# FFN 0 of a layered fp32 backbone on Trainium2: the up projection of seven feature pieces as seven block products

## The reference

```
h = x * (1 + scale) + shift
x = LayerNorm(alpha * x + gate * f(h))          # f: the mixer, then the MLP
_sq_relu_mlp(h, w1, w2) = square(relu(h @ w1)) @ w2      # 1024 -> 4096 -> 1024
```

## Time and profile before

| | us |
|---|---|
| median of three runs | 1986.85 (1986.79 to 1987.31) |
| the profiled execution | 1987.33 |
| its span, first to last instruction | 1985.5 |
| TensorE busy | 1974.4 (99%) |
| VectorE busy | 1257.6 (63%) |
| ScalarE busy | 627.3 (32%) |
| GpSimd busy | 435.5 (22%) |

### The profile page before, as it was taken

One profiled execution on the slowest core, in us unless ns is written; L12 is line 12 of the kernel. 1 busy time (PEld: TensorE's weight loads), 2 busy tenths in 40 slices (PEclk: granted clock), 3 DMA queues, 4 the chain that ended last, 5 costly groups with the idle time before them and its releaser, 6 DMA issues.

```text
span 1985.5 us, 26120 instructions
## 1 busy us (share of the span) xinstructions
PE 1974.4 (99%) x9693; PEld 1696.7 (85%) x9693; DVE 1257.6 (63%) x1783; ACT 627.3 (32%) x897; POOL 435.5 (22%) x350
## 2 busy tenths in 40 slices
PE   9999999999999999999999999999999999999998
PEld 6889889889989988998888888888888888888887
DVE  4756678688656745565783644553554477776778
ACT  3413222144222222222444223313322334444443
POOL 0300311324331233243350020020020026200004
PEclk9999999999999999999999999999999999999999
DMA  9613334332423422333322121212112125877646
GB/s 340 239 64 75 117 117 138 97 96 96 147 97 116 127 95 95 127 125 128 88 95 69 53 91 64 75 64 80 63 65 90 55 85 168 225 218 194 173 147 148
DMA packets 84640, 235.51 MB, mean 119 GB/s; under 512 B 14144, under 2 KB 27072, under 8 KB 84416
## 3 DMA queue, kind: packets, MB, share of 16 engines
q1 hardware_dynamic: 77104, 212.00, 31.9%
q0 software_dynamic: 5616, 18.35, 5.2%
q10 hardware_dynamic: 1824, 3.85, 0.6%
HBM read 219.99 MB, written 2.12 MB: 112 GB/s over the span
## 4 chain that ended last, share of the span: by engine, by line
PE 95%; POOL 1%; DVE 1%; DMA 1%; SPq 1%; issue 1%; ACT 1%; POOLq 0%; ACTq 0%; DVEq 0%
PE bank L863 21%; PE bank L865 21%; PE bank L864 21%; PE bank L901 7%; PE bank L903 7%; PE bank L902 7%; PE bank L1439 2%; PE bank L1442 2%; PE bank L1441 2%; PE bank L1216 1%; PE bank L1167 1%; PE bank L1079 1%; DMA mod<-mod_units_d 0%; PE bank L1051 0%; PE bank L1101 0%
## 5 line engine op out<-in xcount | busy, mean ns | idle before, releaser
L1865 DVE TENSOR_TENSOR w_lo<-raw,w_hi 128x1024 fp32r<-128x1024 f32 x185 | 246.2, 1331 | 325.8 <-ACT w_hi L1465 325.6
L1465 ACT ACTIVATE w_hi<-raw 128x1024 fp32r<-128x1024 f32 x185 | 195.2, 1055 | 561.9 <-PE bank L865 349.2
L863 PE MATMUL bank<-hT_hi,w_hi 128*128 128x384 f32 (+1 forms) x992 | 341.9, 345 | 0.0
L865 PE MATMUL bank<-hT_hi,w_lo 128*128 128x384 f32 (+1 forms) x992 | 340.5, 343 | 0.0
L864 PE MATMUL bank<-hT_lo,w_hi 128*128 128x384 f32 (+1 forms) x992 | 340.5, 343 | 0.0
L2645 POOL TENSOR_TENSOR res_lat<-res_lat,gy 128x512 f32<-128x512 f32 x112 | 149.3, 1367 | 515.3 <-DVE gy L1974 414.9
L901 PE MATMUL bank<-w_hi,hT_hi 128*128 128x512 f32 x592 | 230.6, 389 | 0.0
L902 PE MATMUL bank<-w_lo,hT_hi 128*128 128x512 f32 x592 | 230.3, 389 | 0.0
L903 PE MATMUL bank<-w_hi,hT_lo 128*128 128x512 f32 x592 | 230.3, 389 | 0.0
L863 PE MATMUL bank<-w_hi,act_hi 128*128 128x512 f32 x504 | 198.2, 393 | 0.0
L865 PE MATMUL bank<-w_hi,act_lo 128*128 128x512 f32 x504 | 196.5, 390 | 0.0
(11 more groups left out here) (346 smaller groups left out, 3485.9 us busy)
## 6 DMA issues: line engine op xcount, KB each, us to landing
raw<-w_units_d SPq DMA_DIRECT2D x249, 512.0 KB, 3.3
mod1a<-mod_units_d SPq DMA_DIRECT2D x32, 384.0 KB, 3.8
mod1b<-mod_units_d SPq DMA_DIRECT2D x32, 384.0 KB, 4.1
wsum<-w_units_d SPq DMA_DIRECT2D x24, 512.0 KB, 3.4
bv<-mod_units_d SPq DMA_DIRECT2D x16, 512.0 KB, 3.4
mod<-mod_units_d SPq DMA_DIRECT2D x14, 512.0 KB, 8.2
wsum<-w_units_d POOLq DMA_DIRECT2D x12, 512.0 KB, 7.9
wsum<-wsum POOLq DMA_DIRECT2D x12, 512.0 KB, 5.9
```

The lines of the kernel that those rows point to most:

```text
L863: nc.tensor.matmul(out, s_hi, m_hi, start=first, stop=False)
L865: return nc.tensor.matmul(out, s_lo, m_hi, start=False, stop=last)
L1465: nc.scalar.activation(halves_of(phase, k, i)[0], raw[:, s, :], ACT.Copy).then_inc(hi_done, 1)
L1865: tt(lo, raw[:, s, :], f32(hi), ALU.subtract).then_inc(lo_done, 1)
```

## The change

1. **Seven products.** In the seven later pieces the up projection is a 2 x 2 by 2 x 2 block product (inputs and features of the weights in two halves, inputs and tokens of the activations in two halves) made with seven products in place of eight. Product q: two feature blocks j, 4 input blocks, three matmuls each, 24 of 384 columns; the order is q1, q6, q5, q3, q7, q2, q4, where q2 and q4 add to the open banks of q1 and q7.
2. **Weight sums.** Four of the seven weight operands are T1 to T4, running sums of blocks, made by accumulate DMAs from GpSimd's queue in three slots `wsum0`. A piece has 11 splits in place of 8.
3. **Token operands.** s1, s2, s4 and q7's operand are sums of blocks of the activations, made once in ffn0a: ScalarE copies three blocks' high halves (x21, x22, x11), six accumulate DMAs of 384 KB add the low halves, VectorE sums (`operand0_sum`) and ScalarE and VectorE split the sums (`operand0_hi`, `operand0_lo`). s4 needs four more DMAs.
4. **Combines.** VectorE makes the results from banks and two common sums: `common`, `less_common` and `result` (14 operations of 384 columns and six squares with relu), with ScalarE's relu for q2.
5. **Modulation.** Four slots (mod1); each piece's products go in four or five places of VectorE's order (MOD1_PLACES: 1, 1, 2, 2, 2 in the mixed pieces, 2, 2, 2, 2 in ffn0z); `rows0` stands behind the third unit of the down half in `ffn0`, `cols0` two tiles later.
6. **Residual.** The 12 shift additions become six accumulate DMAs of 512 KB, each issued behind its pair of multiplications in ffn0a. In the heads ScalarE waits for the residual ahead of the copy of the first score.
7. Loops are unrolled; buffers and parities of slots move accordingly.

The core of the diff:

```diff
+PRODUCTS0 = [(1, 6, True), (6, 0, True), (5, 2, True), (3, 0, True), (7, 4, True), (2, 6, False), (4, 4, False)]
...
+MOD1_SEQ = [(g, n) for g in range(PIECES_MIXED) for n in range(KC)]
+for _p, _a, _b in ((3, 0, 2), (4, 2, 5), (5, 5, 8)):
+    MOD1_SEQ += [(_p, n) for n in range(KC)] + [(7, n) for n in range(_a, _b)]
+MOD1_SEQ += [(6, n) for n in range(KC)]
+MOD1_PLACES = [[1, 1, 2, 2, 2]] * 3 + [[1, 2, 2, 2, 3]] + [[1, 2, 2, 3, 3]] * 2 + [[2, 2, 2, 2]]
...
+            def ffn0(p):
+                phase, i = piece0(p)
+                for n, (q, b, opens) in enumerate(PRODUCTS0):
+                    pe.wait_ge(lo_done, before("splits", phase, i) + n + 1)
+                    if p == 0 and q in SLO:
+                        pe.wait_ge(s_lo0, SLO[q])
+                    hi, lo = halves_of(phase, n, i)
+                    x_hi, x_lo = OPERANDS0[q]
+                    for j in range(2):
+                        free(phase, i, f"q{q}.{j}")
+                        out = bank[b + j][:, 0:HALF0]
+                        for kc in range(KC // 2):
+                            w = slice((j * KC // 2 + kc) * P, (j * KC // 2 + kc + 1) * P)
+                            nc.tensor.matmul(out, hi[:, w], x_hi[:, kc, :], start=opens and kc == 0, stop=False,
+                                             skip_group_check=True)
+                            nc.tensor.matmul(out, hi[:, w], x_lo[:, kc, :], start=False, stop=False, skip_group_check=True)
+                            last = nc.tensor.matmul(out, lo[:, w], x_hi[:, kc, :], start=False, stop=kc == KC // 2 - 1,
+                                                    skip_group_check=True)
+                        last.then_inc(pe_step, 1)
...
+                def rows():
+                    pe.wait_ge(mod_used, len(MOD1_SEQ) if phase == "ffn0z" else MOD1_SEQ.index((p, KC - 1)) + 1)
+                    mod_sums(phase, i, "rows0", 6, [macc[:, 0, :], macc[:, 0 if PIECES_MIXED <= p < PIECES_F - 2 else 1, :]],
+                             WIDE_M1 // 2)
...
+                    if phase == "ffn0a" and c == 1:
+                        for dst, k, t in ((x21, first, t_second), (x22, second, t_second), (x11, first, t_first)):
+                            nc.scalar.activation(dst[:, :, :], hT_hi[:, k, t].bitcast(F32), ACT.Copy).then_inc(x_copied, 1)
+                    if phase == "ffn0a" and c == 2:
+                        operand0_hi(1, x22, s1_hi[:, :, :])
+                if phase == "ffn0a":
+                    operand0_hi(2, x21, OPERANDS0[7][0])
+                    split_hi(phase, i, 5, used_unit(phase, i, 3))
+                    operand0_hi(3, x22, s2_hi[:, :, :])
+                    split_hi(phase, i, 6, used_unit(phase, i, 4))
...
+                def result(n):
+                    j, q = n % 2, (3, 7, 2, 4)[n // 2]
+                    if q == 2:
+                        dve.wait_ge(c11_relu, 2 * p + j + 1)
+                        st = stage[:, j, 0:HALF0]
+                        tt(st, bank[6 + j][:, 0:HALF0], st, ALU.mult).then_inc(dve_drain, 1)
+                        return
+                    st = stage_slot(phase, i, n, HALF0)
+                    if q == 3:
+                        done(5, j)
+                    ended(q, j)
+                    if q == 7:
+                        tt(st, d_of(j), bank[4 + j][:, 0:HALF0], ALU.subtract).then_inc(dve_drain, 1)
+                    else:
+                        tt(st, bank[(j, 4 + j)[q == 4]][:, 0:HALF0], (d_of(j), r_of(j))[q == 4], ALU.add).then_inc(dve_drain, 1)
+                    done(q, j)
+                    stt(st, st, 0.0, st, ALU.max, ALU.mult).then_inc(stage_full, 1)
...
+                    result(7)
+                    block0_lo(p, 8)
+                    result_lo(6)
+                    result_lo(7)
+                    products(2)
+                    block0_lo(p, 9)
+                    products(3)
+                    for t in range(TILES0):
+                        drain0(p, 0, t)
+                    block0_lo(p, 10)
+                    products(4)
+                    block0_lo(p + 1, 0)
...
+                    block0_lo(p, 8)
+                    result(7)
+                    products(2)
+                    result_lo(6)
+                    block0_lo(p, 9)
+                    result_lo(7)
+                    block0_lo(p, 10)
+                    products(3)
...
+                    if phase == "ffn0a" and c == 2:
+                        for n in range(3):
+                            dve.wait_ge(x_whole[n], 32)
+                        operand0_sum(1, x22, x21, x22)
+                        operand0_sum(2, x21, x11, x21)
...
+                if phase == "ffn0a":
+                    operand0_lo(1, x22, s1_lo[:, :, :], s1_hi[:, :, :])
+                    split_lo(phase, i, 5)
+                    operand0_sum(3, x22, x22, x11)
+                    dve.wait_ge(pe_step, step_of("ffn0a", 0, "up3.1"))
+                    operand0_lo(2, x21, OPERANDS0[7][1], OPERANDS0[7][0])
+                    operand0_lo(3, x22, s2_lo[:, :, :], s2_hi[:, :, :])
+                    split_lo(phase, i, 6)
...
+            def ln_scale_shift():
+                pool.wait_ge(lnbc_scaled, 1)
+                pool.wait_ge(stage_lo, before("stage", "ln0a") + 2 * KC)
+                for t in range(TILES0):
+                    for h in range(2):
+                        c = slice(h * 512, (h + 1) * 512)
+                        gt(res(t)[:, c], res(t)[:, c], lnbc0[:, 0, c], ALU.mult).then_inc(res_mul, 1)
+                    pool.wait_ge(res_mul, BASE_MUL["ln0a"] + 2 * t + 2)
+                    nc.gpsimd.dma_start(res(t), lnbc0[:, 1, :], accum_op=ALU.add).then_inc(shifted0, 16)
...
+            ln_scale_shift()
+            for n, (dst, k, t) in enumerate(((x21, first, t_second), (x22, second, t_second), (x11, first, t_first))):
+                pool.wait_ge(x_copied, n + 1)
+                add_operand(dst, hT_lo, k, t, x_whole[n])
+            for x in (T3, T1, T2):
+                weight_sum0(0, x)
+            pool.wait_ge(shifted0, 16 * TILES0)
+            pool.wait_ge(s_lo0, 3)
+            add_operand(x22, hT_hi, second, t_first, s4_whole)
+            add0(-1, 0)
+            pool.wait_ge(s4_whole, 32)
+            add_operand(x22, hT_lo, second, t_first, s4_whole)
...
-            for half in range(2):
-                p = PIECES_MIXED + half
-                for h in range(2):
-                    for t in range(TILES0):
-                        add_one("ffn0", p, h, t, TILES0)
-                    shift_some(count("add", "ffn0", p, h * TILES0 + TILES0 - 1), half, range(3 * h, 3 * h + 3))
```

More of the change, by code:

```diff
@@ L639, in weights @@
                 if u >= RAW:
-                    sp.wait_ge(lo_done, i * per + (u - RAW + 1))
+                    more = BASE["heads"]["splits"] - BASE["heads"]["units"] if u >= BASE["heads"]["units"] else 0
+                    sp.wait_ge(lo_done, i * per + (u - RAW + 1 + more))
                 sp.dma_start(raw[:, u % RAW, :], w_units[i * per + u]).then_inc(w_in[u % RAW], 16)
@@ new lines, in load_block0 @@
+            def load_block0(p, x, slot):
+                sp.dma_start(two(raw[:, slot, :]), up_block(p, x)).then_inc(w_in[slot], 16)
+            for k in range(RAW):
+                weights(at + k)
+            load_base0(0, T3)
+            load_base0(0, T2)
+            sp.wait_ge(shifted0, 16 * TILES0)
+            load_base0(0, T1)
+            at = BASE["ffn0"]["units"]
+            sp.wait_ge(lo_done, before("splits", "ffn0a") + 5)
+            load_block0(0, B11, 0)
+            sp.wait_ge(lo_done, before("splits", "ffn0a") + 6)
@@ L777, in _ @@
+            for p in range(PIECES_F - 1):
+                piece_loads(p)
             sp.wait_ge(dve_drain, drained("ffn0z", 0, "cols0")[1])
@@ L908, in token_units, with down @@
                             between[q, t]()
-            def down(phase, i, k0, tiles, a_hi, a_lo, ready, late=None, rows=None, columns=None):
+            def down(phase, i, k0, tiles, a_hi, a_lo, ready, late=None, rows=None, columns=None, rows1=None, columns1=None):
                 for half in range(2):
@@ L1360, in first_units @@
                 for k in range(2):
[L1361 removed]
+                    pe.wait_ge(lo_done, before("splits", "ffn1a") + (k + 1))
                     free("ffn1a", 0, f"up{k}.0")
@@ L1679, in ffn @@
             def ffn(phase, i, groups, width, a_hi):
-                begin = before("step", phase, i)
                 for c in range(CH):
@@ L1721, in ffn, with operand0_hi @@
                     block_hi(0, 1)
[L1722 to L1724 removed]
+            def operand0_hi(n, src, out):
+                act.wait_ge(s_sum0, n)
+                nc.scalar.activation(out, src[:, :, :], ACT.Copy).then_inc(s_hi0, 1)
             ffn("ffn0a", 0, 2, HALF0, act_hi0)
[L1727 to L1729 removed]
+            for p in range(PIECES_F - 1):
+                ffn0(p)
             scale_lnbc(1, lnbc0)
@@ L2711, in _, with add_operand, add0 @@
```

(8 more changed lines are left out.)

519 lines of the change are left out of this document (368 added, 151 removed).

## The result

The changed kernel takes 2036.55 us (2035.22 to 2037.83, 4 runs) against 1986.82 before; the ratio is 1.025, with a 95% interval from 1.0232 to 1.0267. The range given ended at 2012. The profiled execution took 2037.83 us, 50.5 more than that of before.

What follows compares the result with a forecast made beforehand. TensorE, busy 1974.4 of 1985.5 us, was taken as the bound. From 1987.3: -29.1 matmuls, +21.7 operand wait, +0.4, +8.3 and +6.0 at rows0, +2.3 clock gave 1996.9, forecast as 1997 us, range 1983 to 2012.

Steps and rivals of the forecast that it cites:

- 168 matmuls removed: Up halves of the seven later pieces: 24 fewer matmuls each at 0.1734 us, -29.1 us.
- wait for unit 5 in ffn0a: TensorE waits in ffn0a's down half for unit 5's w_lo, behind the operand sums: +21.7 us.
- operands in piece 0 (q6): Piece 0: s2's low half is slightly late for product q6, +0.4 us; the other operands are in time.
- rows0, mixed pieces: Three mixed pieces: TensorE waits 2.8 us each at rows0 for the eighth modulation product, +8.3 us.
- rows0, ffn0z: Last piece: TensorE reaches rows0 34.6 us in, VectorE's last products end at 40.4, +6.0 us.
- slow clock: TensorE runs for a while at 1.2 GHz after the long wait and four short ones: +2.3 us (0 to 6).
- Step 2 of the operand sums: In ffn0a the six operand transfers, at the software queue's 178 GB/s, are whole at 510, taken as 511.
- rival B: Accumulates go one at a time, GpSimd stopping at each issue; operands whole at 518 to 528, 2004 to 2015 us; chance 0.2.
- Steps 1, 3 and 4: ffn0a: last shift issued at 492; 9.0 us from operands' arrival to unit 5's w_lo; TensorE needs it at 498.31.
- Rival A: ffn0a's operand transfers overlap and land by 501.5; 12 us wait, 1986 us, or 1973 with products in time; chance 0.2.
- Rival C: VectorE becomes the bound: w_lo of q2 and q4 1 to 2 us late in each piece, 2004 to 2011; chance 0.1.
- D: The change is not what it says; the order shows the 168 matmuls in all seven pieces, so no chance given.

Runs made afterwards that it cites:

- no_low_dmas: The changed kernel without the six accumulate DMAs that add low halves to x21, x22 and x11: 2006.35 us.
- unit5_first: The changed kernel with the operand wait and two sums moved behind unit 5's w_lo in ffn0a, order alone: 2035.75 us.
- rows_later: The changed kernel with rows0 4.1 us later, cols0 two tiles after it, and ffn0z's last two modulation products earlier on VectorE: 2019.11 us.

## Why the prediction was wrong

Most terms of the sum were right in kind. Three were too small, and two waits were missing from it: of the 40.9 us between forecast and measurement 18.3 are the wait for unit 5, 12.5 the slow clock and 8.1 the missing waits.

| term of the prediction | forecast | in the profiled execution |
|---|---|---|
| 168 matmuls removed | -29.1 | -29.1 (168 fewer instructions, at the forecast's price) |
| wait for unit 5 in ffn0a | +21.7 | +40.0 |
| operands in piece 0 (q6) | +0.4 | +2.0 |
| rows0, mixed pieces | +8.3 | +9.2 |
| rows0, ffn0z | +6.0 | +5.5 |
| slow clock | +2.3 | +14.8 |
| gy, behind the residual additions | 0 | +5.6 |
| ScalarE's copies ahead of a bank copy | 0 | +2.5 |
| sum | +9.6 | +50.5 |

- **Step 2 of the operand sums is the one that failed.** It took the queue's mean rate, 178 GB/s, and laid the six transfers end to end, whole at 510 to 511. The rate was right: the queue moved 40.11 MB in 11.6% of 2036 us, 170 GB/s. But an issue waited until the queue had room, so between two transfers there was idle time: 4.7 us for 384 KB, 84 GB/s. They were whole at 532, 4 us beyond the upper end of 518 to 528. The mechanism is that of rival B, which had 0.2 and a price of 2004 to 2015; that price missed the measured time by 21 us too, as it had neither the wait for `gy` nor most of the clock's 14.8. Its rows were among those read: the issues that waited 4.65 and 9.30 us were for 512 KB in long packets, and the operands have 272 packets each, 144 where rows are long. I chose by the mean over the program in place of the nearest rows, those with an issue that waits. Nor were those rows the same case: from 1700 to 1725 the DMA engines were busy 96% of the time, while in ffn0a they stood idle between the transfers.
- **Steps 1, 3 and 4 hold.** The last shift was issued at 495 against 492. From arrival to TensorE it was 9.0 us, as added up. TensorE stood at 501.2 in place of 498.3, as 2.5 us were lost at 484: ScalarE's three copies (4.22 us in a row) stand ahead of the bank copy there. The prediction added up VectorE's and GpSimd's orders in ffn0a, and not ScalarE's.
- **What is queued behind GpSimd's waits was left out.** The residual additions stand behind three weight sums and s4's first pair. The prediction named the queue only for the operands. That is the wait of 5.6 us here, of 17.5 us in no_low_dmas and of 8.0 us in unit5_first.
- **The modulation sums** came out at 14.7 us against 14.3, and rows_later removed what it should.
- **The slow clock** was priced at 2.3 us for the long wait and four short ones. The long one alone cost 2.0, and six of the seven short ones 1.7 to 2.9 each: 14.6 us in all. rows_later, by some 8 us for the four at `rows0`, agrees. Pieces 3 to 5, which have no wait, follow each other at 63.2 us as forecast, the mixed ones at 67.9.
- **Rival A** (quick transfers) is refuted: landing took a median of 4.4 us, and the next operand DMA was not issued beside it. The rule of the Trainium skill that went with this rival (DMA: Bandwidth & Descriptors, section Anatomy of one DMA - SWDGE (gpsimd) path), 2.9 us for 384 KB as an estimate, does not hold here: the bytes moved at 155 to 182 GB/s in the stretches above, where the rule has 436. **Rival C** did not show: after q6 of piece 0 no product waited for its `w_lo`. **D**: the 168 matmuls are gone.

## What to carry to other kernels

Here a DMA issued by GpSimd cost room in its queue as well as its bytes: read the spacing of issues that waited, from a stretch where several follow each other, and count the packets of the new ones. Ask of every wait put into an in-order queue what stands behind it; here the same queue carried the residual additions, so that removing the first wait only showed the second. A short wait of TensorE mostly cost 1.7 to 2.9 us more than its length here (and nothing behind one of 2.50 us, or behind the 3.1 us of rows_later), so small ones add up: the four at `rows0` were 14.7 us of waiting and 8.0 of slow clock. Moving the consumer a little later can be the cheapest edit.

## What was unexpected of the hardware

- Accumulate DMAs of 272 packets (1536-byte rows) went one at a time, 4.7 us apart for 384 KB, though the data of one took about 2.3 (by 170 GB/s). With 144 packets each (3072-byte rows) three were issued back to back, and the sums of the operands started 13.7 us earlier.
- A DMA instruction on GpSimd takes 1.20 us with 272 packets and 0.89 with 144.
- The granted clock fell to 0.50 during the wait of 40 us and stayed there for 4.0 us of work after it; after a wait of 5.6 us it was 0.50 for 5.8 us. After one of 3.1 us it was 0.51 for 3.5 us, and after one of 1.98 us 0.57 over the next 4.0, but after one of 2.50 us it did not fall. So what follows a wait can't be told from its length alone.
- In the changed kernel nothing but TensorE's waits and its clock explains the 50.5 us: waits, slow clock and removed matmuls leave 0.2 us. Whether the exact room of the queue is a number of packets or of bytes of descriptors stays open.
